# Output projection of a streaming conv mixer on one core: direct products against seven products of half operands per pair of row tiles

## What is computed

```
hn = rms_norm(x, norm_g);  proj = hn @ w_in            # 1024 -> 3584
h_a, b_a, c_a, z_a, a_b, g_b, z_b = split(proj, 512 each)
out_a = b_a * conv3(c_a * h_a) * silu(z_a)
conv_b = conv31(a_b * sigmoid(g_b)) + bias
out_b = silu(layer_norm(conv_b)) * silu(z_b)           # LayerNorm over 512 channels
y = rms_norm(x + concat(out_a, out_b) @ w_out, final_norm_g)
```

## Time and profile before

| | us |
|---|---|
| median of 3 runs | 1552.09 |
| lowest, highest | 1551.67, 1553.0 |
| span of the profiled execution | 1551.4 |
| TensorE busy | 1540.5 (99%) |
| VectorE busy | 1271.0 (82%) |
| GpSimd busy | 577.2 (37%) |
| ScalarE busy | 539.5 (35%) |
| output stage, 1180.5 to 1537.1 | 356.6 |

### The profile page before, as it was taken

The page is one execution under the profiler, slowest core; times in us unless marked ns, Lnnn a source line. Parts: engine busy times, 40 slices in busy tenths (PEclk is TensorE's granted clock), DMA queues, the critical chain, the costliest instruction groups (busy, mean ns, idle before and its releaser), DMA issues.

```text
span 1551.4 us, 19357 instructions
## 1 busy us (share of the span) xinstructions
PE 1540.5 (99%) x7282; PEld 1359.1 (88%) x7282; DVE 1271.0 (82%) x1179; ACT 539.5 (35%) x793; POOL 577.2 (37%) x495
## 2 busy tenths in 40 slices
PE   9999999999999999999999999999999999999998
PEld 8999999888888888888888888888898888888886
DVE  7699999988877997869798887789896677787753
ACT  5453442332341333332253312234533332323322
POOL 2886869011313121232221141146964233332310
PEclk9999999999999999999999999999999999999999
DMA  6898787788987778887779777647645433444432
GB/s 240 327 360 315 289 316 256 283 282 280 316 260 241 233 256 309 291 287 242 235 223 306 253 241 246 213 172 225 206 119 186 177 119 138 178 162 176 156 129 82
DMA packets 111352, 361.64 MB, mean 233 GB/s; under 512 B 17172, under 2 KB 21268, under 8 KB 107680
## 3 DMA queue, kind: packets, MB, share of 16 engines
q1 hardware_dynamic: 111264, 360.47, 69.1%
HBM read 266.63 MB, written 93.80 MB: 232 GB/s over the span
## 4 chain that ended last, share of the span: by engine, by line
PE 81%; DVE 2%; issue 0%; ACT 0%; POOL 0%; POOLq 0%; DVEq 0%; ACTq 0%
PE ps L2003 27%; PE ps L2005 27%; PE ps L2004 27%; DVE ps L1771 1%; DVE xf L1601 0%; PE ps L2114 0%; PE ps L2113 0%; PE ps L2135 0%; PE ps L2128 0%; DVE h_rows L1932 0%; DVE h_rows L1935 0%; DVE h_rows L1929 0%; DVE h_rows L1918 0%; DVE ps L1768 0%; ACT ps L1540 0%
## 5 line engine op out<-in xcount | busy, mean ns | idle before, releaser
L1771 DVE SCALAR_TENSOR_TENSOR ps<-v,conv_b_taps,ps 128x920 f32<-128x920 f32 (+2 forms) x580 | 630.8, 1088 | 17.8
L2003 PE MATMUL ps<-xf,w_ring 128*128 128x460 f32 (+1 forms) x1624 | 603.1, 371 | 1.5 <-issue 1.2
L2005 PE MATMUL ps<-xf,w_ring 128*128 128x460 f32 (+1 forms) x1624 | 602.6, 371 | 0.0
L2004 PE MATMUL ps<-xf,w_ring 128*128 128x460 f32 (+1 forms) x1624 | 600.8, 370 | 0.0
L2003 PEld LDWEIGHTS ps<-xf,w_ring 128*128 128x128 f32 x1624 | 305.4, 188 | 36.3 <-issue 2.9
L2004 PEld LDWEIGHTS ps<-xf,w_ring 128*128 128x128 f32 x1624 | 305.4, 188 | 34.0
L2005 PEld LDWEIGHTS ps<-xf,w_ring 128*128 128x128 f32 x1624 | 304.9, 188 | 34.2
L1318 ACT ACTIVATE sets<-ps 128x460 f32<-128x460 f32 x168 | 92.8, 552 | 488.7 <-PE ps L2005 488.5
L1112 POOL TENSOR_TENSOR sets<-sets 128x460 f32<-128x460 f32 x42 | 56.3, 1341 | 418.2 <-ACT sets L1318 418.2
L2003 PE MATMUL ps<-w_out_split,mixed 128*128 128x512 f32 x512 | 199.7, 390 | 0.0
L2004 PE MATMUL ps<-w_out_split,mixed 128*128 128x512 f32 x512 | 199.4, 390 | 0.0
(11 more groups left out here) (170 smaller groups left out, 1679.9 us busy)
## 6 DMA issues: line engine op xcount, KB each, us to landing
w_ring<-weight_forms SPq DMA_DIRECT2D x294, 512.0 KB, 4.8
x_rows_again<-in_x_prompt SPq DMA_DIRECT2D x32, 512.0 KB, 4.2
out_y_prompt<-h_rows SPq DMA_DIRECT2D x32, 512.0 KB, 3.0
x_raw<-in_xT SPq DMA_DIRECT2D x32, 460.0 KB, 6.7
weight_forms<-xf SPq DMA_DIRECT2D x7, 2048.0 KB, 13.1
weight_forms<-w_ring SPq DMA_DIRECT2D x7, 2048.0 KB, 12.5
w_ring_f<-in_w_in SPq DMA_DIRECT2D x56, 256.0 KB, 3.2
xf_f<-in_w_in SPq DMA_DIRECT2D x26, 512.0 KB, 6.4
```

Of the source, the lines that this page charges most:

```text
L1771: dve.scalar_tensor_tensor(dst, window, wb[:, j, k:k + 1], part, ALU.mult, ALU.add).then_inc(taps_done, 1)
L2003: pe.matmul(out, ahi, bhi, start=(start and x == 0), stop=False, skip_group_check=goes_on)
L2004: pe.matmul(out, ahi, blo, start=False, stop=False, skip_group_check=goes_on)
L2005: mm = pe.matmul(out, alo, bhi, start=False, stop=(stop and x == len(terms) - 1), skip_group_check=goes_on)
```

## The change

- **Output stage by pairs.** Two row tiles (256 rows) and two halves of the channels (out_a, out_b) are treated as a 2x2 of quarters, W_out as well. Seven products of sums replace eight: 16 pairs x 7 products x 12 matmuls of 512 columns. Products stay in PSUM banks and go on in them (P1, P6, P7, P4 in one, P5, P3 in another, P2 in a third), and after each of the seven VectorE adds the bank to one half of a row tile that holds x (`add_product`).
- **Operand forms.** VectorE makes four sums for a pair (`form_sums`), ScalarE seven high halves (`form_high_of`), GpSimd seven low halves (`form_low`), each 512 columns, in eight places used in turn. `a_low`, `b_low` and ScalarE's two big copies go.
- **LayerNorm.** Column sums and spreads for all blocks; the second mean and the Newton steps go. Its steps stand in slots of the 14 products of two pairs (`ln_slot`).
- **W_out's forms** are made in periods 15 to 45 of the middle units (`form_step`): SP loads raw rows to ring places 1 and 2, ScalarE makes the high half, GpSimd the sum and the low half in place 3, SP stores 512 KB; 28 of them. In the late unit SP loads 24 of them back, the four of P4 after it.
- **Ring.** Six places instead of nine.
- **Squares** of rows by halves, four a pair; root with one more operation. Sample rows: 40 matmuls instead of 32.
- Everything written out, without the loop.

The diff's core ("+" and "-" as in the change):

```diff
+PAIRS = SEQ // (2 * P)
+ACC_BANK, STAT_BANK, SQUARE_BANK = 6, 7, 6
 FIRST_BANK = 7
 HI_ORDER = [0, 1, 3, 2, 4, 5, 6]
+RING = [4, 5, 6, 7, 8, 0]
+DEEP = len(RING)
+RAW_E, RAW_F, STAGE = 1, 2, 3
+OUT_FORMS = [P1, P2, P3, P5, P7, P6, P4]
+FORM_STEPS = JT * len(OUT_FORMS)
+FORM_PERIODS = len(OUT_FORMS) + 1
+OUT_ADDS = {P1: (0, 0), P5: (1, 1), P6: (0, 1), P2: (0, 0), P7: (1, 1), P3: (0, 1), P4: (1, 0)}
+FORM_PLACES = 8
+LAST_BANKS = [(3, 4), (5, 7)]
...
+def form_step(n):
+    e, j = divmod(n - II - 1, FORM_PERIODS)
+    return (e, j) if 0 <= e < JT and j < len(OUT_FORMS) else None
...
         def slot_of(q):
-            return (q + 4) % 9
+            return RING[q % DEEP]
         def weights_in(q):
-            return 16 * (q // 9 + 1)
+            return 16 * (q // DEEP + 1)
...
+        def wait_form_free(eng, m, i):
+            f = form_at(m, i)
+            if f >= FORM_PLACES:
+                eng.wait_ge(out_done, f - FORM_PLACES + 1)
+            elif f < 5:
+                eng.wait_ge(half_done, 52 + f)
+            elif f < 7:
+                eng.wait_ge(half_done, 4 * G14)
             else:
-                eng.wait_ge(arrived[s], 8 * (L - s) + 16 * s)
+                eng.wait_ge(form_lo, form_at(0, P1) + 1)
+                eng.wait_ge(sums_made, 4)
...
+        def ln_slot(L, step):
+            if L == 1:
+                return {"sums": 1, "sum_low": 3, "mean": 4, "centre": 4, "squares": 5, "square_sums": 6, "columns": 7,
+                        "spread": 8, "normalise": 9, "silus": 10, "gate": 11}[step]
+            return {"mean": 1, "centre": 2, "squares": 3, "square_sums": 4, "columns": 5, "spread": 7,
+                    "normalise": 9, "silus": 10, "gate": 11}.get(step)
...
+        def sums_now(m, i, step):
+            if m < 2 and ln_slot(1, step) == 7 * m + i:
+                return 1
+            if m // 2 + 2 <= OBLOCKS and 7 * (m % 2) + i == {"sums": 11, "sum_low": 13}[step]:
+                return m // 2 + 2
+            return None
...
+                if q >= DEEP:
+                    sp.wait_ge(product_done, q - DEEP + 1)
...
+            def store_out_form(e, j):
+                sp.wait_ge(wr_lo, form_done(e, j))
+                dst = out_forms_d[OUT_FORMS[j]].rearrange("p (e l m) -> p e l m", e=JT, l=2)[:, e]
+                sp.dma_start(dst, ring[:, STAGE, :, :].bitcast(F32)).then_inc(wr_out, 16)
+            def make_out_forms(n):
+                if form_step(n - 1):
+                    store_out_form(*form_step(n - 1))
+                if form_step(n + 1) and form_step(n + 1)[1] == 0:
+                    load_out_raw(form_step(n + 1)[0])
...
+            def load_out_form(i, e):
+                if i == P1 and e == 0:
+                    sp.wait_ge(product_done, PRODUCTS)
+                    sp.wait_ge(x8_lo, 2)
+                    sp.wait_ge(wr_out, 16 * FORM_STEPS)
+                src = out_forms_d[i].rearrange("p (e l m) -> p e l m", e=JT, l=2)[:, e]
+                to = wf4[:, e, :, :] if i == P4 else wf[:, i, e, :, :]
+                sp.dma_start(to.bitcast(F32), src).then_inc(wf_in[i], 16)
...
+            def form_low(m, i):
+                f = form_at(m, i)
+                pool.wait_ge(form_hi, f + 1)
+                if i in (P5, P6):
+                    pool.wait_ge(sums_made, 4 * m + (2 if i == P5 else 3))
+                of = {P1: out_a(m)[0], P2: out_b(m)[0], P4: out_b(m)[1]}.get(i)
+                pool.tensor_tensor(form_part(m, i, 1), form_part(m, i, 1, True) if of is None else of,
+                                   form_part(m, i, 0).bitcast(F32), ALU.subtract).then_inc(form_lo, 1)
...
+            for m in range(PAIRS):
+                for i in range(7):
+                    if m and i == 0:
+                        row_rstd(m - 1, 0)
+                        form_low(m, P7)
+                        row_rstd(m - 1, 1)
+                    if m == 0 and i == 0:
+                        form_low(0, P5)
+                        form_low(0, P6)
+                        form_low(0, P2)
+                        form_low(0, P7)
+                    if i == 1:
+                        form_low(m, P3)
+                    if i == 2:
+                        form_low(m, P4)
+                    if m + 1 < PAIRS:
+                        if i == 4:
+                            form_low(m + 1, P1)
+                        if i == 5:
+                            form_low(m + 1, P5)
+                        if i == 6:
+                            form_low(m + 1, P6)
+                            form_low(m + 1, P2)
+                    if ln_now(m, i, "columns"):
+                        column_rstd(m // 2 + 1)
+                    if sums_now(m, i, "sums") is not None:
+                        sums(sums_now(m, i, "sums"))
+                    if sums_now(m, i, "sum_low") is not None:
+                        sum_low(sums_now(m, i, "sum_low"))
...
+            def out_form_high(e, j):
+                f = form_done(e, j) - 1
+                need(act, wr_out, 16 * f)
+                if j < 3:
+                    act.wait_ge(wr_in, 32 * (e + 1))
+                else:
+                    act.wait_ge(wr_sum, JT * e + j - 2)
+                of = {P1: ring_f32[:, RAW_E, 0, :], P2: ring_f32[:, RAW_F, 0, :], P3: ring_f32[:, RAW_F, 1, :],
+                      P5: ring_f32[:, STAGE, 1, :], P7: ring_f32[:, RAW_E, 1, :], P6: ring_f32[:, RAW_E, 0, :],
+                      P4: ring_f32[:, RAW_F, 0, :]}[OUT_FORMS[j]]
+                act.activation(ring[:, STAGE, 0, :], of, ACT.Copy).then_inc(wr_hi, 1)
...
+            for m in range(PAIRS):
+                for i in range(7):
+                    if m == 0 and i == 0:
+                        form_high_of(0, P5)
+                        form_high_of(0, P6)
+                        form_high_of(0, P2)
+                        form_high_of(0, P7)
+                    if m and i == 0:
+                        half_square(m - 1, P3)
+                        half_square(m - 1, P4)
+                    if i == 0:
+                        form_high_of(m, P3)
+                    if i == 1:
+                        form_high_of(m, P4)
+                    if sums_now(m, i, "sum_low") is not None:
+                        sum_high(sums_now(m, i, "sum_low"))
+                    if ln_now(m, i, "squares"):
+                        squares(m // 2 + 1)
+                    if ln_now(m, i, "columns"):
+                        column_var(m // 2 + 1)
+                    if m + 1 < PAIRS and i == 4:
+                        form_high_of(m + 1, P1)
+                    if i == 5:
+                        half_square(m, P2)
+                    if m + 1 < PAIRS and i == 5:
+                        form_high_of(m + 1, P5)
+                        form_high_of(m + 1, P6)
+                    if i == 6:
+                        half_square(m, P7)
+                    if m + 1 < PAIRS and i == 6:
+                        form_high_of(m + 1, P2)
+                        form_high_of(m + 1, P7)
+                    if ln_now(m, i, "silus"):
+                        silus(m // 2 + 1)
...
+            def form_sums(m, names):
+                a11, a21 = out_a(m)
+                a12, a22 = out_b(m)
+                made = lambda i: form_part(m, i, 1, True)
+                for i in names:
+                    wait_form_free(dve, m, i)
+                    if i == P5:
+                        wait_out_a(dve, m)
+                        dve.wait_ge(ln, ln_event(m // 2, "gated"))
+                        dve.tensor_tensor(made(P5), a21, a22, ALU.add).then_inc(sums_made, 1)
+                    if i == P6:
+                        dve.wait_ge(sums_made, 4 * m + 1)
+                        dve.tensor_tensor(made(P6), made(P5), a11, ALU.subtract).then_inc(sums_made, 1)
+                    if i == P3:
+                        dve.wait_ge(sums_made, 4 * m + 2)
+                        dve.tensor_tensor(made(P3), a12, made(P6), ALU.subtract).then_inc(sums_made, 1)
+                    if i == P7:
+                        dve.tensor_tensor(made(P7), a11, a21, ALU.subtract).then_inc(sums_made, 1)
...
+            def add_product(m, i):
+                to = h_part_of(m, i)
+                dve.wait_ge(out_done, added(m, i))
+                if i in (P1, P5, P6, P4):
+                    dve.wait_ge(x_rows_in[m % 2], 32 * (m // 2 + 1))
+                else:
+                    dve.wait_ge(h_add, added(m, {P2: P1, P7: P5, P3: P6}[i]))
+                dve.tensor_tensor(to, ps[:, bank_of_product(m, i), :], to, ALU.add).then_inc(h_add, 1)
...
+            form_sums(0, [P3, P7])
+            for m in range(PAIRS):
+                for i in range(7):
+                    if i:
+                        add_product(m, i - 1)
+                    elif m:
+                        add_product(m - 1, P4)
+                    if m and i in (1, 2):
+                        finish_rows(m - 1, i - 1)
+                    if ln_now(m, i, "centre"):
```

(37 more changed lines are left out.)

859 lines of the change are left out of this document (401 added, 458 removed).

## The result

| | before | after |
|---|---|---|
| median of the runs, us | 1552.55 (4 runs) | 1594.84 (4 runs) |
| lowest, highest | 1551.67, 1555.73 | 1594.43, 1597.67 |
| ratio, 95% interval | | 1.0273 (1.0255 to 1.0290) |
| span of the profiled execution | 1551.4 | 1592.6 |
| TensorE busy | 1540.5 (99%) | 1530.3 (96%) |

What follows compares the result with a forecast made beforehand. TensorE, busy 1540.5 of 1551.4 us, was taken as the bound, with VectorE/GpSimd sharing making it wait. 1551.4 + 24.8 + 0.6 + 1.5 + 1.9 + 1 = 1581.2, plus 0.7 to the median: 1582; eight-in-ten range 1536 to 1600.

Steps and rivals of the forecast that it cites:

- Products, LayerNorm on TensorE: Output stage: 192 fewer matmuls save 43.5 us; with LayerNorm's changes TensorE does 40.3 us per block, if nothing waits.
- The exclusion: Output stage: VectorE's two-SBUF-input operations and all GpSimd's share one resource, waiting for each other's whole operation; 40.5 us per block.
- It cannot run without gaps, so TensorE will wait.: Output stage: 40.5 us of shared VectorE/GpSimd resource per 40.3 us of TensorE leaves gaps, because operations hang on one another.
- The chain from E: From E, the end of P5 of a block's second pair: mean at E+21.8, waits 5.5 plus 2.8, 8.3 us a block.
- Stage: Output stage: blocks of 49.1, six of 48.6 and 40.7 us make 381.4 against 356.6, +24.8 us.
- Clock: Output stage: TensorE's waits may lower its granted clock; 0 to 12 us, 1 taken.
- The case that I hung on the page: Output stage: repeated waits throttle TensorE each time, costing 12 us, time 1593; chance 0.15 out of the forecast's.
- Start of the stage: First pair's P5 waits for its operand halves, +0.6 us; P4's late-loaded weights cost 0, at most 3.
- Middle units: W_out's form steps delay the chain at both unit edges: 1.5 us taken, 0 to 6 given.
- Ring of six: Rival: with six places, loads landing over 12.2 us beside the stores starve the products; 1597 to 1612, chance 0.05.
- Late unit, tail: Late unit loses low halves and loads forms: 0, 0 to 2 us; tail's eight more sample matmuls: +1.85 us.
- the marks set down beforehand: Right: waits at mean and column sums, 7 to 9 us a block, GpSimd near 75%. Wrong: stage clock under 1.

Runs made afterwards that it cites:

- the run with the new places: Changed kernel with LayerNorm's steps, row finishes and row roots at other places in the engines' lists, same instructions: 1536.28 us, ratio 0.9901 to the kernel before.
- run with PSUM inputs: Changed kernel with one SBUF input of VectorE's four form sums per pair replaced by a PSUM bank (sums' values wrong): 1579.43 us, ratio 1.0180 to the kernel before.
- side-by-side run: Changed kernel plus nine sections of VectorE and GpSimd operations, alone or together, behind its last store; four two-SBUF-input operations on each together took 6.8 us.
- with the clock held: Changed kernel with matmuls nobody reads put on TensorE where it waited in the output stage: 1586.58 us, ratio 1.0229 to the kernel before.
- the run with the mean later: Changed kernel with LayerNorm's mean, centring, squares, column sums and spread two products later from the second block on: 1590.73 us, ratio 1.0266 to the kernel before.

## Why the prediction was right, and where it was off

The sign held, and so did the mechanism in the stage, a chain of single operations that makes TensorE wait at the mean and at the column sums. The time was 12.8 us short of 1594.8, which lies near the upper ends of the ranges given (1597 and 1600): the clock and the middle units were under-sized. By its steps:

- **Products, LayerNorm on TensorE.** Right. In the run with the new places, where TensorE hardly waits, a block holds 40.6 to 40.8 us of TensorE's work; the step had 40.3.
- **The exclusion.** Right in kind (run with PSUM inputs, side-by-side run) and nearly in size: 10.1 us of the stage for one input of the sums, 12 expected. A turn of both is 1.7 us (6.8/4) against 0.55 + 1.1 = 1.65.
- **"It cannot run without gaps, so TensorE will wait."** This sentence was wrong as a reason. The kernel with other places does the same exclusive work, 40.5 us by the count, in blocks of 41.4 us. The waits came from where the operations stood.
- **The chain from E.** Right to 0.5 us: mean at E+22.1 (21.8 by the text; its terms, 9.9 + 10.1 + 1.6, give 21.6), column sums at the mean's start +14.0 (+14.1). TensorE came to the mean at E+17 instead of E+16.3 and waited 4.9 instead of 5.5; at the column sums 1.0 instead of 1.8, at P7 0.2 instead of 1.0, because its products in between ran at the low clock and it came later.
- **Stage.** 381.4 forecast; 382.8 with the clock held, 389.4 as it is. First block 51.4, or 48.0 with the clock held (49.1), last 40.9 (40.7), those between 48.9 and 50.1 (48.6). The same lists took 392.2 in another execution.
- **Clock.** The term that was mis-sized most in the stage: 1 taken, 0 to 12 given, 6.6 measured (9.4 by the other execution). The granted clock fell in each of the first seven blocks, not in some. By the page TensorE: Matmul & The Clock Gate of the Trainium skill (Part 1, HAM oscillation) repeated waits throttle TensorE each time; the trace agrees, with a fall at each of the six waits of about 5 us. With shorter ones it is not each time: in the run with the mean later, a block with waits of 2.6 and 2.0 us stayed at 1.00 (1331.5 to 1377.2). The case that I hung on the page said 12 us and had 0.15 of the chance; it should have been the forecast's own mechanism at half to three quarters of that price, because a chain of other engines runs beside the slow matmuls. That its 1593 lies within 2 us of the measured time is luck: the clock cost less than its 12 us, and the middle units made up for it.
- **Start of the stage.** +0.6 forecast, no wait measured. The weights of P4 cost nothing, as said.
- **Middle units.** 1.5 taken, 0 to 6 given, 9.2 in the profiled execution and 3.0 to 6.0 in five others with the same forms in the same places: under-sized in all of them. The edges cost 3.9 (1.1 and 2.8): the mechanism was named, GpSimd beside VectorE's low halves, but two operations fell into one edge. The other 5.3 (periods 44 and 45) was not in the sum at all: I followed who waits for SP and for the ring, and not that ScalarE's high half waits for the store of the form before with the copy of P7 behind it. The step left out was to ask of every added wait, ScalarE's too, what is queued behind it.
- **Ring of six.** The rival fell: TensorE's waits for the ring's loads are none in the changed kernel and 0.5 us where the other middle waits are gone. Loads of the ring took 3.5 to 14.3 us to land, median 5.4; the prediction had 12.2 as the turning point, and even those above it cost nothing.
- **Late unit, tail.** 0 and +1.9 forecast; -0.5 (two mean matmuls gone, overlooked) and +1.7 measured.
- **Unit 0 and the median.** The profiled execution was 2.0 us faster up to unit 1, and the median was 2.2 over that execution's span where I added 0.7. Both are differences between executions.

Together: stage with its start and clock 32.8 instead of 26.4, so 6.4 more; middle 7.7 more; unit 0, late unit and tail 2.7 less; median 1.5 more: 12.9, against 12.8 between forecast and median.

Of the marks set down beforehand: the waits stood at the two places named, with 6.1 us a block instead of 7 to 9; GpSimd was busy 67% of the stage (262.4 of 389.4), not 75%; low halves were 1.52 us and the last form sum 1.77. A granted clock under 1 in the stage had been named as a sign against me, and it was there.

## What to carry to other kernels

A change that takes work from the busiest engine and gives more, smaller steps to the others is decided by where those steps stand in the engines' lists: lay one repetition out on all engines with measured durations, ask for every wait which operation stands behind it, and move the steps before judging the idea. After moving one late step, look for the chain that is late next; here the first fix alone gave 4 us, no more than executions differ by, and the full set 59. When an engine that waits loses clock, count that only as far as nothing slower runs beside it. And take the price of a stage from more than one profile: here the same lists cost 3 us in the middle in one execution and 9 in another.
